# Three more row pairs of the FFN's second product computed by block products, with the sums of its weight blocks made by DMAs

## The reference

```
h = rmsnorm(x, norm_ffn_pre[layer])
gate, up = jnp.split(h @ w_ffn_in[layer], 2, axis=-1)
x = x + rmsnorm((jax.nn.silu(gate) * up) @ w_ffn_out[layer], norm_ffn_post[layer])
```

## Time and profile before

| | |
|---|---|
| median of 3 runs | 916.75 us |
| profiled execution, own time | 916.93 us |
| its span | 915.2 us |
| PE busy | 905.9 us (99%), 5254 matmuls |
| DVE, ACT, POOL busy | 636.1, 488.7, 159.0 us |
| DMA | 113.67 MB, mean 124 GB/s |
| granted TensorE clock | full, 0.999 of 2.4 GHz as the mean |

### The profile page before, as it was taken

One profiled execution on the slowest core, in us unless ns is written; L12 is line 12 of the kernel. 1 busy time (PEld: TensorE's weight loads), 2 busy tenths in 40 slices (PEclk: granted clock), 3 DMA queues, 4 the chain that ended last, 5 costly groups with the idle time before them and its releaser, 6 DMA issues.

```text
span 915.2 us, 14402 instructions
## 1 busy us (share of the span) xinstructions
PE 905.9 (99%) x5254; PEld 798.1 (87%) x5254; DVE 636.1 (70%) x1179; ACT 488.7 (53%) x926; POOL 159.0 (17%) x168
## 2 busy tenths in 40 slices
PE   8999999999999999999999999999999999999997
PEld 8888888888888888888888888989999999988885
DVE  5998655462555556556567758768888888679786
ACT  6744245433566666667754445445565555424762
POOL 3000264344133424344510001000000000000000
PEclk9999999999999999999999999999999999999999
DMA  9323627232323232374236743113223322480002
GB/s 347 122 74 88 199 92 221 79 93 93 109 75 110 76 115 88 110 257 139 89 133 257 288 143 111 47 48 128 103 93 114 117 93 93 156 344 7 13 12 92
DMA packets 37602, 113.67 MB, mean 124 GB/s; under 512 B 4324, under 2 KB 6948, under 8 KB 36780
## 3 DMA queue, kind: packets, MB, share of 16 engines
q1 hardware_dynamic: 36700, 109.08, 34.4%
q10 hardware_dynamic: 832, 3.67, 1.3%
HBM read 98.87 MB, written 13.66 MB: 123 GB/s over the span
## 4 chain that ended last, share of the span: by engine, by line
PE 97%; DVE 1%; issue 1%; DMA 1%; ACT 0%; SPq 0%; DVEq 0%; POOLq 0%; POOL 0%; ACTq 0%
PE bank L2209 27%; PE bank L2211 27%; PE bank L2210 27%; PE bank L821 3%; PE bank L813 2%; PE bank L838 2%; PE bank L836 2%; PE bank L812 2%; PE bank L2274 1%; PE bank L2228 1%; DMA xT<-x_features 1%; PE bank L2403 0%; PE bank L2461 0%; PE bank L752 0%; PE bank L2324 0%
## 5 line engine op out<-in xcount | busy, mean ns | idle before, releaser
L1095 ACT ACTIVATE w_hi<-w_raw 128x1024 fp32r<-128x1024 f32 (+1 forms) x90 | 94.7, 1053 | 127.2 <-PE bank L2211 123.7
L2209 PE MATMUL bank<-h_hi,w_lo 128*128 128x512 f32 x352 | 139.9, 397 | 0.0
L2210 PE MATMUL bank<-h_lo,w_hi 128*128 128x512 f32 x352 | 137.5, 391 | 0.0
L2211 PE MATMUL bank<-h_hi,w_hi 128*128 128x512 f32 x352 | 137.4, 390 | 0.0
L1511 DVE TENSOR_TENSOR w_lo<-w_raw,w_hi 128x1024 fp32r<-128x1024 f32 (+1 forms) x69 | 84.3, 1224 | 42.3 <-ACT w_hi L1095 42.1
L705 DVE CUSTOM_DVE_ANT_0 sc<-bank,fullb 128x512 f32<-128x512 f32 (+1 forms) x96 | 47.0, 490 | 77.7 <-PE bank L813 75.9
L605 ACT ACTIVATE sc<-sc,ast 128x512 f32<-128x512 f32 (+1 forms) x96 | 53.9, 561 | 72.8 <-DVE ast L705 72.7
L1037 POOL TENSOR_TENSOR sc<-sc,ast 128x512 f32<-128x512 f32 (+1 forms) x96 | 66.3, 722 | 130.7 <-DVE ast L727 97.7
L2211 PE MATMUL bank<-tx_hi,op_hi 128*128 128x256 f32 x288 | 81.5, 283 | 0.0
L2210 PE MATMUL bank<-tx_lo,op_hi 128*128 128x256 f32 x288 | 81.5, 283 | 0.0
L2209 PE MATMUL bank<-tx_hi,op_lo 128*128 128x256 f32 x288 | 81.5, 283 | 0.0
(11 more groups left out here) (381 smaller groups left out, 2438.2 us busy)
## 6 DMA issues: line engine op xcount, KB each, us to landing
w_raw<-wpack SPq DMA_DIRECT2D x132, 512.0 KB, 3.6
gate_logits<-gl_out SPq DMA_DIRECT2D x24, 256.0 KB, 2.2
gl_in<-gate_logits SPq DMA_DIRECT2D x24, 256.0 KB, 5.2
dn_sw<-wpack SPq DMA_DIRECT2D x4, 1536.0 KB, 9.7
near_bias<-near_bias ACTq DMA_DIRECT2D x1, 2880.0 KB, 13.3
xT<-x_features SPq DMA_DIRECT2D x8, 256.0 KB, 5.8
xs<-x_in SPq DMA_DIRECT2D x4, 512.0 KB, 8.7
fullb<-near_bias SPq DMA_DIRECT2D x16, 128.0 KB, 3.1
```

What stands on the lines that cost most here:

```text
L1095: sa.activation(split_weights(c)[0][:, 0:n], raw[:, s, 0:n], ACT.Copy).then_inc(w_hi, 1)
L2209: mm(out, ll, rh, start=start, stop=False, skip_group_check=True)
L2210: mm(out, lh, rl, start=False, stop=False, skip_group_check=True)
L2211: return mm(out, lh, rh, start=False, stop=stop, skip_group_check=True)
```

## The change

- Nine pairs (three groups of three) instead of six go through block products: `DOWN_GROUPS = 3`, 21 operands instead of 14; four plain tiles are left instead of ten.
- The second product's weights of those pairs lie in DRAM by block (b11, b12, b21, b22). The right-hand sums t1 to t4 are no longer made by DVE: in attention POOL issues eight DMAs from DRAM to DRAM, four copies and four with `accum_op=ALU.add`, each of 288 rows of 2048 floats (2304 KB), at units 6, 22, 38, 54, 70 and 86, with a wait for the DMAs before each step after the first.
- Each operand's right block (768 KB) is loaded by SP into one of five slots, the sixth and later ones when PE is done with operand o - 5. SP's first load waits for `sums_in` and for the last use of `h_hi` in the first product. The load of `wfpost` stands in the same queue.
- The left-hand sums are made by DVE after the last plain tile (s1 after the last but one), and three signs change.
- `z_mean` is one instruction (the 1/D goes into the scale of the square) and stands ahead of `z_weight`; `plain_into_c21(0)` stands between the two `z_out`s.
- Tiles have other addresses; six more activation tiles take part in the sums.

The diff, cut to what the text speaks of:

```
-DOWN_PAIRS = 3
+DOWN_PAIRS, DOWN_GROUPS = 3, 3
+N_DOWN = DOWN_PAIRS * DOWN_GROUPS
-F_DOWN = NF - 4 * DOWN_PAIRS
+F_DOWN = NF - 2 * N_DOWN
+RIGHT_RAW, DOWN_HI = 5, 4
...
+        sums_dram = nc.dram_tensor("down_sums", (4, N_DOWN * BLOCK), F32, kind="Internal").ap()
...
+        def right_landed(eng, o):
+            eng.wait_ge(load_in[o % RIGHT_RAW], 16 * (o // RIGHT_RAW + 2))
...
-            for c in range(C_OUT + RAW_SLOTS, C_FOUT + 6):
+            def load_right(o):
+                i, g = divmod(o, DOWN_GROUPS)
+                if o >= RIGHT_RAW:
+                    sp.wait_ge(dn_done, operand_done(o - RIGHT_RAW))
+                mine = down_blocks[DOWN[i][1]][g * DOWN_PAIRS * BLOCK:(g + 1) * DOWN_PAIRS * BLOCK]
+                sp.dma_start(dn_right[o % RIGHT_RAW][:, :, :], mine.rearrange("(j p n) -> p j n", j=DOWN_PAIRS, p=P)
+                             ).then_inc(load_in[o % RIGHT_RAW], 16)
+
+            for c in range(C_OUT + RAW_SLOTS, C_DOWN):
                 fetch(c)
-            sp.wait_ge(op_used, N_OPERANDS)
-            load_group(0)
-            fetch(C_FOUT + 6)
-            load_group(1)
-            for c in range(C_FOUT + 7, C_DOWN):
-                fetch(c)
+            sp.wait_ge(op_used, used_at(operand(N_PAIRS - 1, "s4")))
+            sp.wait_ge(sums_in, 128)
+            for o in range(2 * DOWN_GROUPS + 2):
+                load_right(o)
             for m in range(2):
                 product_done(sp, 1, m)
             sp.dma_start(wfpost[:, :], rows_d[2, :, :]).then_inc(posts_in, 16)
+            for o in range(2 * DOWN_GROUPS + 2, DOWN_GROUPS * len(DOWN)):
+                load_right(o)
...
+            def down_add(name, of):
+                pool.dma_start(down_blocks[name], down_blocks[of], accum_op=ALU.add, max_dma_last_dim=8192
+                               ).then_inc(sums_in, 16)
             for u in range(len(UNITS) + 8):
+                if u == 6:
+                    down_copy("t1", "b11")
+                    down_copy("t3", "b12")
+                elif u == 22:
+                    pool.wait_ge(sums_in, 32)
+                    down_add("t1", "b12")
+                    down_add("t3", "b22")
+                elif u == 38:
+                    pool.wait_ge(sums_in, 64)
+                    down_copy("t2", "t3")
+                elif u == 54:
+                    pool.wait_ge(sums_in, 80)
+                    down_add("t2", "b11")
...
                 if u < len(UNITS):
                     scale(u)
...
-            down_high(12)
+            for o in range(16, 19):
+                down_high(o)
             z_square(0, 0)
             z_square(1, 0)
-            down_high(13)
+            for o in range(19, 21):
+                down_high(o)
             copy_out(5, 0, 2)
...
-                link(ve.tensor_tensor(stat[:, t:t + 1], stat[:, 56 + 2 * t:57 + 2 * t],
-                                      stat[:, 57 + 2 * t:58 + 2 * t], ALU.add))
-                ve.tensor_scalar(stat[:, 36 + t:37 + t], stat[:, t:t + 1], 1.0 / D, EPS, ALU.mult,
-                                 ALU.add).then_inc(norm_ms, 1)
+                ve.tensor_scalar(stat[:, 36 + t:37 + t], stat[:, 56 + 2 * t:57 + 2 * t], stat[:, 57 + 2 * t:58 + 2 * t], EPS,
+                                 ALU.add, ALU.add).then_inc(norm_ms, 1)
```

More of the change, by code:

```diff
@@ L313, in program @@
[L313 to L319, removed]
@@ L320, in program @@
-        junk_z = at(24, "junk_z", [P, 512])
+        dn_left, dn_left_low = {}, {}
+        for n, name in enumerate(("s1", "s2", "s4")):
+            dn_left[name] = at(168 + 9 * n, f"dn_{name}", [P, N_DOWN, 256])
+            dn_left_low[name] = at(168 + 9 * n, f"dn_{name}_low", [P, N_DOWN, 256], F32R)
+        dn_right = [at(6 * k, f"dn_right{k}", [P, DOWN_PAIRS, 512]) for k in range(RIGHT_RAW)]
+        dn_right_low = [at(6 * k, f"dn_right_low{k}", [P, DOWN_PAIRS, 512], F32R) for k in range(RIGHT_RAW)]
@@ new lines, in program @@
+        dnh_left = [at(195 + 3 * k, f"dn_left_hi{k}", [P, DOWN_PAIRS, 256], F32R) for k in range(DOWN_HI)]
+        dnh_right = [at(144 + 6 * k, f"dn_right_hi{k}", [P, DOWN_PAIRS, 512], F32R) for k in range(DOWN_HI)]
+        kept = [at(120 + 2 * i, f"kept{i}", [P, SEQ]) for i in range(4)]
+        copied = [at(32 + 2 * i, f"copied{i}", [P, SEQ]) for i in range(4)]
+        zn = at(48, "zn", [P, 2, D])
+        wfpost = at(56, "wfpost", [P, D])
+        junk_z = at(60, "junk_z", [P, 512])
+        down_flat = wpack[C_DOWN:N_CHUNKS, :, :].rearrange("c p n -> (c p n)")
@@ L1398, in down_high @@
                     summed(sa, left, g)
-                else:
[L1400 to L1412, removed]
-                    sa.wait_ge(w_used, count(C_DOWN - 1) + 1)
-                sa.activation(dnh_right[o % 4][:, :, :], down_right(right, g), ACT.Copy).then_inc(dn_hi, 1)
+                if o < DOWN_HI:
+                    sa.wait_ge(f_free, NF + 2)
+                    sa.wait_ge(op_used, N_OPERANDS)
+                else:
+                    sa.wait_ge(dn_done, operand_done(o - DOWN_HI))
+                sa.activation(dnh_left[o % DOWN_HI][:, :, :], down_left(left, g), ACT.Copy)
+                right_landed(sa, o)
+                sa.activation(dnh_right[o % DOWN_HI][:, :, :], dn_right[o % RIGHT_RAW][:, :, :], ACT.Copy).then_inc(dn_hi, 1)
             def keep(i, b):
@@ L2137, in _ @@
                 lo(C_FOUT + k)
-                for name, g in between.get(k, ()):
-                    down_sum(name, g)
-            for o in range(5):
+                if k == 2:
+                    for g in range(DOWN_GROUPS):
+                        down_sum("s1", g)
+            for name in ("s2", "s3"):
+                for g in range(DOWN_GROUPS):
+                    down_sum(name, g)
+            for o in range(3):
+                down_low(o)
+            for g in range(DOWN_GROUPS):
+                down_sum("s4", g)
+            for o in range(3, 6):
                 down_low(o)
@@ L2178, in _ @@
             z_weight(1, 1)
-            down_low(12)
+            for o in range(16, 19):
+                down_low(o)
+            z_mean(0)
             z_weight(0, 0)
-            z_mean(0)
+            z_mean(1)
             z_weight(1, 0)
-            z_mean(1)
-            down_low(13)
+            down_low(19)
+            down_low(20)
             z_out(0, slice(0, D))
+            plain_into_c21(0)
             z_out(1, slice(0, D))
-            plain_into_c21(0)
             plain_into_c21(1)
@@ L2614, in down_block @@
                 left, right = DOWN[i]
-                o = 2 * i + g
-                high, low = dnh_left[o % 4], down_left(left, g, True)
-                wide, narrow = dnh_right[o % 4], down_right(right, g, True)
+                o = DOWN_GROUPS * i + g
+                high, low = dnh_left[o % DOWN_HI], down_left(left, g, True)
+                wide, narrow = dnh_right[o % DOWN_HI], dn_right_low[o % RIGHT_RAW]
                 out = bank[(2, 4, 2, 4, 0, 2, 2)[i] + m]
@@ L2629, in down_block @@
                     last = three(out[:, :], high[:, j, mine], low[:, j, mine], wide[:, j, :], narrow[:, j, :],
[L2630 removed]
+                                 i < 2 and g == 0 and j == 0, g == DOWN_GROUPS - 1 and j == DOWN_PAIRS - 1)
                 last.then_inc(dn_done, 1)
             for i in range(len(DOWN) - 1):
[L2634 removed]
+                for g in range(DOWN_GROUPS):
                     for m in range(2):
@@ L2637, in _ @@
             for m in range(2):
-                for g in range(2):
+                for g in range(DOWN_GROUPS):
                     down_block(len(DOWN) - 1, g, m)
@@ L2697, in pack_weights @@
         out.append(tiles(a["w_ffn_in"][0][:, HID * side + P * f:HID * side + P * f + P]))
-    rows = list(range(F_DOWN))
-    rows += [F_DOWN + 2 * (DOWN_PAIRS * g + j) + k for g in range(2) for k in range(2) for j in range(DOWN_PAIRS)]
-    for k in rows:
+    for k in range(F_DOWN):
         out.append(a["w_ffn_out"][0][P * k:P * k + P])
+    blocks = a["w_ffn_out"][0][P * F_DOWN:].reshape(N_DOWN, 2, P, 2, 512).transpose(1, 3, 0, 2, 4)
+    out.extend(np.ascontiguousarray(blocks).reshape(2 * N_DOWN, P, CHUNK))
     for c, m in enumerate(out):
```

134 lines of the change are left out of this document (56 added, 78 removed).

## The result

The changed kernel takes 939.6 us (median of 4 runs, 936.02 to 942.67) against 916.66 us for the kernel before (4 runs, 916.06 to 920.31): ratio 1.024, 95% interval 1.022 to 1.026. It is 2.4% slower. The forecast was 916.0 us with a range to 922, so it was wrong.

A forecast was written before the change was run, and what follows sets the result against it. PE was taken to bound the kernel (busy 99% of the span). Terms -4.1 + 0.1 + 1.7 + 2.3 - 0.8 + 0 = -0.8 us gave a median of 916.0 us; 911.9 to 919 with its bounds, range up to 922.

The forecast's parts named there:

- Matmuls removed: Second product: three pairs go from 48 plain to 42 block matmuls each, 18 fewer in all at 0.2267 us: -4.1 us.
- The start of the block products: After the four plain tiles, PE waits for DVE's six sums and first remainders: +0.1 us (0 to 1).
- The load for operand 8: Second product's third group: the load queues behind wfpost, so PE waits: +1.7 us (1.1 to 4.7).
- The seventh product: Before product 6, PE waits 2.9 us for plain_into_c21(0) behind operand 20's remainder; 0.6 before, so +2.3 us.
- rival 1: Full gain: neither second-product wait is there, as loads land faster or DVE adds before the last remainder; 911.3 us, chance 0.14.
- The tail: Kernel end, from ACT's last square to the first z_out: one tiny op goes first while zn runs beside it; -0.8 us.
- The DMAs in attention: POOL's DRAM copies and adds fit free DMA time; adds cost 1.5 copies, PE feels them only from 1.96: 0 us.
- rival 2: Attention: adds at 2.5 times a copy hold POOL at unit 38 and PE for 12 us; 928 us, chance 0.17.
- Rival 3: Attention: POOL issues each DMA slowly, 4 us each, so pairs at units 6 and 22 overrun: +5.6, 921.6 us, chance 0.05.

The follow-up runs named there:

- the version with both orders changed: Changed kernel with sums made in the input stage, wfpost loaded behind operand 12, and plain_into_c21(0) ahead of operand 20's remainders: 911.99 us, ratio 0.9952.

## Why the prediction was wrong

- **Matmuls removed**, -4.1: right. 5236 matmuls, and where -4.1, -0.6 and -0.8 were all that counted (-5.5) the time was 5.1 us below the kernel before, 911.99 us for 911.8 expected.
- **The start of the block products**, +0.1: right; no row of PE waits there.
- **The load for operand 8**, +1.7: right in place, cause and length (1.87 us). The fit of the Trainium skill (DMA: Bandwidth & Descriptors, Anatomy of one DMA), by which the forecast reckons 1.3 us, is one to DMAs issued by GpSimd, and this load is issued by SP.
- **The seventh product**, 2.9 us: right (2.79 us), and its remedy is the order that rival 1 supposed.
- **The tail**, -0.8: right within 0.1 (-0.7).
- **What no term had**: PE's clock after a wait. In the profiled execution of the changed kernel it cost 3.3 us in the second product, and most of the 7.4 us by which PE was busy longer in attention. Without a fall the forecast's sum for the second product is nearly met: -0.1 in the run without the sums, for -0.8. Every wait was priced at its length, and by the medians costs 1.1 to 1.6 us more.
- **The DMAs in attention**, 0: this step failed, by 21 us. Its sums on POOL were right: issuing cost 0.6 to 1.3 us for one, each DMA was back before the next step, and no row of POOL waits for them. The pair of adds took 1.48 times as long as the pair of copies (29.3 and 19.8 us), the 1.5 that the forecast took from the bytes, and far from the 1.96 that rival 2 needed. What failed is the sentence on the stores: "2.2 us, have some 5.5 us before ACT needs `gl_out` again". The slack was right, at its shortest 7.6 us from issue to need in the kernel before; the 2.2 us were read where the DMA share was 0.29. Beside an add it was 10.5 to 12.4 us. The swaps of `ckx`, for which the forecast has no term, made 5.8 us of PE's waits. By the forecast's own sign (attention's length changes by over 1 us) it is wrong, by 21.2.
- **The range of the forecast itself**: the bounds given with its terms add up to 914.0 to 920.6 us, not to the 911.9 to 919 that stand beside its chance. 939.6 lies outside either.
- **Rival 2** named the adds and 928 us, but by another way (POOL's queue at unit 38), which no run shows. **Rival 3** (issue slow) is refuted by POOL's rows. **Rival 1** is what the version with both orders changed shows, 911.99 us for 911.3, once the DMAs are out of attention. In the changed kernel itself both waits are there.

The Trainium skill has a rule that would have spoken against the step (DMA: Bandwidth & Descriptors, Queues, rings and completion order): each DMA engine takes turns between queues by whole packets of several descriptors, and from this it follows that a small store waits for turns of the bulk transfer beside it. The first store's 10.6, 8.3 and 8.0 us beside adds in rows of 8, 4 and 2 KB agree in direction; no run here separates the size of a packet from the time that an add takes in it.

Open: why adds move only 215 GB/s on engines that are as busy as with copies (343 GB/s at a share of 0.98 beside the second pair of plain copies), and why some pauses of the same length are followed by a slow clock and others aren't. Neither was settled.

## What to carry to other kernels

Work that "fits" in free DMA bandwidth must also be checked against the deadline of every small transfer that shares the engines: list the transfers that some engine waits for, with time from issue to need, and multiply their quiet latency by five to six, not by one (10.5 to 12.4 us here for 2.1 to 2.2). If bulk traffic can go to a stage without such deadlines, put it there; if not, shorter rows or no accumulation took 14 to 17 of the 23 us away here. And price a new pause of TensorE above its length.

## What was not expected of the hardware

- An accumulating DMA within DRAM, 2304 KB, took 15.4 to 15.5 us alone and a pair 29.3 us, against 10.0 us for a lone copy and 19.8 for a pair; the DMA share beside the pair of adds was 0.96 at 215 GB/s.
- Beside an add a 256 KB store took 10.5 to 12.4 us instead of 2.1, and beside plain copies alone 7.3 to 10.5 us (15.7 us where the loads of `ob` and `gl_in` stood beside the copy too).
- Cutting the same DMAs into rows of 4 KB instead of 8 KB gave 922.65 us instead of 939.6, with the adds themselves slower (17.7 us in the median for 15.5).
- Behind pauses of 1.8 to 2.0 us and of 2.8 us TensorE's granted clock went to 0.50, for 3.4 or 6.8 us, in three of eight and in six of nine profiles, and stayed at 1.00 in the others. In four of eleven it also stood at 0.50 for 3.4 us in the input stage, where PE had not paused.
